# The first norm of a hybrid network taken in token rows ahead of the turn

## The chip, the cores and the metric

The kernel runs on one core of one Trainium2 chip. The metric is the device time of one execution in microseconds. Busy time, granted clock of TensorE and transfers are those of one profiled execution.

## What is computed

A network of two layers over 1,024 tokens of width 1,024, all in 32-bit floats. The part that matters here is its very start, the norm of the input and the first product with `hy_w_in`:

```
def rms_norm(x, w):
    xf = x.astype(jnp.float32)
    y = xf * lax.rsqrt(jnp.mean(xf * xf, axis=-1, keepdims=True) + EPS)
    return (y * w.astype(jnp.float32)).astype(x.dtype)
...
    h = x
    for layer in range(DEPTH):
        e = layer // 2
        y = rms_norm(h, norm_mix[layer])
        if layer % 2 == 0:
            y = hybrid_mixer(y, hy_w_in[e], ...)     # begins with y @ w_in
        else:
            y = nsa_mixer(y, nsa_w_in[e], ...)
        h = h + y
        h = h + conv_ffn(rms_norm(h, norm_ffn[layer]), ...)
    return rms_norm(h, norm_final)
```

Each token's row is divided by its root mean square, and each of its 1,024 features is then scaled by a gain. The raw `x` is needed again, as the residual, only after the mixer.

## The kernel before

Activations lie turned in SBUF: features on the 128 partitions, tokens along the row. `H` holds 8 such tiles (MT = 8, `H[:, m, :]`) of 128 features by 1,024 tokens. Products are made in units. A unit is one block of 128 output features; TensorE goes over i = 0 to 7 and for each i issues six matmuls of 512 columns. Both factors are split into an upper and a lower part (`WH`, `WL` of the weights, `YH`, `YL` of the normed activations), and three products of the parts are summed. GpSimd (POOL) splits the weights, `WH` (line 473) and `WL` (line 476), one unit of weights at a time into one of two slots; SyncE (SP) loads them into `WR` (line 376). Unit n's split waits for the end of unit n-1 on TensorE once both slots are in use, and the load of unit n waits for the split of unit n-2.

The start runs in this order. SP loads `x` as 8 tiles of 128 tokens into `Z`, then two small gate weight blocks (`GWR`), then the weights of units 0 and 1. The ACT queue issues 14 small parameter loads (`par_pieces`) and 6 small vector loads. TensorE turns the parameters (line 1876), VectorE (DVE) copies them to `PTF` (lines 1220, 1221). TensorE turns raw `x` (line 1883), 8 transposes for each m, into two pairs of PSUM banks; ACT copies the even tiles to `H` (line 803), DVE the odd ones (line 1224). Then ACT squares each tile (line 756), DVE adds the squares (lines 1135, 1137), TensorE sums over the partitions (line 1862), ACT takes the root (line 758), DVE the reciprocal (line 1143), and TensorE spreads the factor over all partitions (line 1869). Per tile m DVE then scales (line 1151), ACT makes `YH` (line 763) and POOL makes `YL` (line 498), through two temporary tiles. Unit 0 follows tile by tile; behind it TensorE makes the gate columns (line 1895), then unit 1, the turned gates, the key squares (line 2080), unit 2 and so on.

Seven level masks `LV` (128x128 each, lines 1247 to 1249) are made by DVE after the norm. The turned raw input `H` is spilled to DRAM as `xt_scratch` (line 404) as soon as the turns are evacuated, and SP issues the weights of unit 2 behind the spill.

There is no planner: each engine follows its own written order, and semaphores join them.

Of the kernel before, what the change touches and what calls it, by code (L numbers as in the profile page):

```python
# [6 lines left out]
def hybrid_nsa_program(nc, x, norm_mix, norm_ffn, norm_final, hy_w_in, gdn_conv, gdn_a_log, gdn_dt_bias,  # L7
# [6 lines left out]
    P = 128  # L14
# [29 lines left out]
    with ctx:  # L44
# [154 lines left out]
        SQ_READY, SQ_USED, SS_READY = (0, MT + 3 * (MT - 1)), (0, MT + 3 * (MT - 2)), (0, 1 + 3 * 2)  # L199
# [26 lines left out]
        (w_split, gemm_done, psum_free, x_loaded, par_loaded, vec_loaded, gw_loaded, gw_split, consts, par_t, pt_ready,  # L226
         xt_ready, xt_used, sq_ready, sq_used, ss_ready, rt_ready, yf_ready, yh_ready, y_ready, rstd_ready, rb_ready,
         spilled, restored_first, restored, xt_used_odd, w_hi, act_chain, dve_chain, pool_chain) = [sem(n) for n in (
             "w_split gemm_done psum_free x_loaded par_loaded vec_loaded gw_loaded gw_split consts par_t pt_ready "
             "xt_ready xt_used sq_ready sq_used ss_ready rt_ready yf_ready yh_ready y_ready rstd_ready rb_ready "  # L230
             "spilled restored_first restored xt_used_odd w_hi act_chain dve_chain pool_chain").split()]
        (tap_ready, conv_act, key_sq, key_ss, key_scale, key_root, gp_ready, sm_a, sm_v, gam_ready, lv_ready, ij_ready) = [sem(n) for n in (
            "tap_ready conv_act key_sq key_ss key_scale key_root gp_ready sm_a sm_v gam_ready lv_ready ij_ready").split()]
# [126 lines left out]

        block = ctx.enter_context(nc.Block())
# [3 lines left out]
        def _(sp):  # L365
            for tt in range(TT):
                sp.dma_start(Z[:, tt, :], x[0, chunk(tt), :]).then_inc(x_loaded, 16)
            w_in = hy_w_in[0].rearrange("(k p) n -> p k n", p=P)
            sp.dma_start(GWR[:, :, 0:8], w_in[:, :, 2048:2056]).then_inc(gw_loaded, 16)
            sp.dma_start(GWR[:, :, 8:16], w_in[:, :, 3592:3600]).then_inc(gw_loaded, 16)  # L370
# [30 lines left out]
            sp.wait_ge(xt_ready, MT)  # L401
# [49 lines left out]
        def _(pool):  # L451
# [42 lines left out]
            def y_lower(r, y0):  # L494

                for m in range(MT):
                    pool.wait_ge(yh_ready, r * MT + m + 1)
                    pool.tensor_tensor(YL[:, m, :], X[:, 17 + m % 2, :], YH[:, m, :].bitcast(f32),
                                       ALU.subtract).then_inc(y_ready, 1)

# [7 lines left out]

            splits(U_QKV, 2)
            gate_split(32, 16)  # L510
            y_lower(0, 0)
# [32 lines left out]
            pool.wait_ge(lv_ready, 1)  # L544
# [195 lines left out]
        def _(act):  # L740
# [7 lines left out]
            def norm(r, n0=None):  # L748
                for m in range(MT):
                    if n0 is None:  # L750
                        act.wait_ge(xt_used if m % 2 == 0 else xt_used_odd, m // 2 + 1)
                    else:
                        act.wait_ge(psum_free, n0 + m + 1)
                    if m >= 2:
                        act.wait_ge(sq_used, SQ_USED[r] + m - 1)
                    act.activation(X[:, 16 + m % 2, :], H[:, m, :], ACT.Square).then_inc(sq_ready, 1)
                act.wait_ge(ss_ready, SS_READY[r] + 1)
                act.activation(RSTD[:, :], PS[:, 4, 0:TT], ACT.Sqrt, scale=1.0 / DM, bias=EPSC[:, 0:1]).then_inc(rt_ready, 1)

            def norm_upper(r):  # L760
                for m in range(MT):
                    act.wait_ge(yf_ready, r * MT + m + 1)
                    act.activation(YH[:, m, :], X[:, 17 + m % 2, :], ACT.Copy).then_inc(yh_ready, 1)

            def half_norm(k, n0):

                for m in range(MT - 1):
                    act.wait_ge(psum_free, n0 + m + 1)
                    if m >= 3:
                        act.wait_ge(sq_used, MT + 6 * k + m - 2)  # L770
                    act.activation(X[:, 16 + m % 2, :] if m else PSF[:, 6 * HALF:8 * HALF], H[:, m, :], ACT.Square).then_inc(sq_ready, 1)
                act.wait_ge(nh_res, k + 1)
                act.wait_ge(sq_used, MT + 6 * k + 5)
                act.activation(X[:, 17, tok_half(0)], H[:, MT - 1, tok_half(0)], ACT.Square).then_inc(nh_sq, 1)

                def root(a):
                    act.wait_ge(ss_ready, 1 + 2 * k + a + 1)
# [4 lines left out]
                for a in range(2):  # L782
                    for m in range(MT):
                        act.wait_ge(yf_ready, MT + (2 * k + a) * MT + m + 1)
# [7 lines left out]
            for dst, src in par_pieces:  # L792
                act.dma_start(dst, src).then_inc(par_loaded, 16)
            for dst, src, lo in ((ALOG, gdn_a_log, 0), (ALOG, ssd_a_log, GH), (DTB, gdn_dt_bias, 0), (DTB, ssd_dt_bias, GH)):
                n = src.shape[1]
                act.dma_start(dst[:, lo:lo + n], src[0].partition_broadcast(P)).then_inc(vec_loaded, 16)
            for half in range(2):
                act.dma_start(DSK[half * 64:half * 64 + 64, :], ssd_d[0, half::2].partition_broadcast(64), allow_slow_non_contiguous=True).then_inc(vec_loaded, 16)


            for m in range(0, MT, 2):
                act.wait_ge(xt_ready, m + 1)
                act.activation(H[:, m, :], gemm_ps(0), ACT.Copy).then_inc(xt_used, 1)
            norm(0)
            norm_upper(0)

# [25 lines left out]
            for n in range(7):  # L832
# [22 lines left out]
                if n < 4:  # L855
                    act.wait_ge(conv_act, n + 1)
                    if n == 0:
                        act.wait_ge(spilled, 16)
                    if n >= 2:
                        act.wait_ge(key_ss, n - 1)  # L860
                    act.activation(X2(HF, 4 + n % 2), X[:, QKV[n], :], ACT.Square).then_inc(key_sq, 1)
# [259 lines left out]
        def _(dve):  # L1121
# [7 lines left out]
            def norm_sums(r, m):  # L1129
# [3 lines left out]
                dve.wait_ge(sq_ready, SQ_READY[r] + m + 1)  # L1133
# [5 lines left out]
                dve.wait_ge(sq_used, SQ_USED[r] + m + 1)  # L1139

            def norm_factor(r):
                dve.wait_ge(rt_ready, r + 1)
                dve.reciprocal(RSTD[:, :], RSTD[:, :]).then_inc(rstd_ready, 1)
                dve.wait_ge(rb_ready, r + 1)

            def norm_apply(r, wcol, y0):
                norm_factor(r)
                for m in range(MT):
                    if m >= 2:
                        dve.wait_ge(y_ready, y0 + m - 1)  # L1150
                    dve.scalar_tensor_tensor(out=X[:, 17 + m % 2, :], in0=H[:, m, :], scalar=PTF[:, wcol + m:wcol + m + 1],
                                             in1=PSF[:, 4 * HALF:6 * HALF], op0=ALU.mult, op1=ALU.mult).then_inc(yf_ready, 1)

            def half_residual(k, n0, wcol):

                def add_square(m):
                    dve.wait_ge(sq_ready, MT + 7 * k + m + 1)
                    dve.tensor_tensor(PSF[:, 6 * HALF:8 * HALF], PSF[:, 6 * HALF:8 * HALF], X[:, 16 + m % 2, :], ALU.add).then_inc(sq_used, 1)
                    dve.wait_ge(sq_used, MT + 6 * k + m)
# [5 lines left out]
                def factor(a):  # L1165
                    dve.wait_ge(rt_ready, 1 + 2 * k + a + 1)
                    dve.reciprocal(RSTD[:, 4 * a:4 * a + 4], RSTD[:, 4 * a:4 * a + 4]).then_inc(rstd_ready, 1)

                def apply(a, m):
                    if m == 0:  # L1170
                        dve.wait_ge(rb_ready, 1 + 2 * k + a + 1)
# [50 lines left out]
            for m in range(1, MT, 2):  # L1222
                dve.wait_ge(xt_ready, m + 1)
                dve.tensor_copy(H[:, m, :], gemm_ps(1)).then_inc(xt_used_odd, 1)

            for m in range(MT):
                norm_sums(0, m)
            norm_apply(0, C_MIX, 0)
# [15 lines left out]
            dve.wait_ge(y_ready, MT)  # L1244
            link(dve.tensor_scalar(LT, UT[:, :], -1.0, 1.0, ALU.mult, ALU.add))
            for l in range(7):
                link(dve.tensor_scalar(XI[:, 1, :], XI[:, 0, :], l, None, ALU.logical_shift_right))
                link(dve.tensor_copy(LV[:, l, :], XI[:, 1, :]))
                ins = dve.scalar_tensor_tensor(out=LV[:, l, :], in0=LV[:, l, :], scalar=1.0, in1=LT,
                                               op0=ALU.is_equal, op1=ALU.mult)  # L1250
                if l < 6:
                    link(ins)
                else:
                    ins.then_inc(lv_ready, 1)
            dve.wait_ge(pt_ready, 2)
# [84 lines left out]
            for n in range(7):  # L1340
                qkv_taps(n)
                if n == 0:
                    dve.wait_ge(gt_ready, 1)
                    dve.wait_ge(spilled, 16)
                    dve.tensor_copy(X2(HF, 7)[0:16], PSF[0:16, 6 * HALF:8 * HALF]).then_inc(gt_sb, 1)
# [26 lines left out]
                if n == 4:  # L1372
# [4 lines left out]
                    link(dve.tensor_tensor(BR2, BETA[:, :, 0:GH], KEYR2, ALU.mult))  # L1377
                    differences(0)
# [162 lines left out]
            def final_gain(m):  # L1541

                dve.wait_ge(sq_ready, SQ_READY[1] + m + 1)
                dve.tensor_scalar(H[:, m, :], H[:, m, :], PTF[:, C_FIN + m:C_FIN + m + 1], None, ALU.mult).then_inc(fin_ready, 1)

            def residual(n0):
                for m in range(MT):
# [228 lines left out]
        def _(pe):  # L1776
# [26 lines left out]
            def half_spread(k, a):  # L1803
                pe.wait_ge(rstd_ready, 1 + 2 * k + a + 1)
# [54 lines left out]
            def norm_sum(r):  # L1859
                pe.wait_ge(sq_used, SQ_USED[r] + MT)  # L1860
# [3 lines left out]
                if r == 1:  # L1864
                    return

                pe.wait_ge(rstd_ready, r + 1)
                for tt in range(TT):
                    ins = pe.matmul(PSF[:, 4 * HALF + tt * P:4 * HALF + (tt + 1) * P], RSTD[:, tt:tt + 1].broadcast_to([P, P]), IDENT[:, :],
                                    start=True, stop=True)  # L1870
                ins.then_inc(rb_ready, 1)
# [6 lines left out]
            pe.wait_ge(x_loaded, 16 * TT)  # L1878
            for m in range(MT):
# [643 lines left out]
```

## Time and profile before

| | |
|---|---|
| median of the runs | 3157.39 us (3147.24, 3157.39, 3164.39) |
| the profiled execution: its own time | 3148.27 us |
| its span | 3146.6 us, 1.7 us less than its own time |
| mean granted clock of TensorE | 0.97 |
| busy: TensorE, VectorE, ScalarE, GpSimd | 2922.7, 1237.2, 952.5, 1402.7 us |
| TensorE stops turning raw `x` | 27.2 us after the span's start |
| first matmul of unit 0 | 52.8 us |
| first gate column | 70.9 us |

The last three lines are read from the timeline of the start. They part the start into the turn of the raw input, the norm, and unit 0.

### The profile page before, as it was taken

How to read it: one execution, taken by the hardware profiler on the slowest of the kernel's cores; microseconds unless marked ns; L12 is line 12 of the kernel's file. 1: busy time of each engine (PE TensorE's matmuls, PEld its weight loads, DVE VectorE, ACT ScalarE, POOL GpSimd, SP SyncE). 2: the span in 40 equal slices, each digit the busy share in tenths (PEclk: the TensorE clock that was granted, in tenths of full speed). 3: DMA queues.
4: the chain of work that ended last, by engine and by line, in shares of the span. 5: the costliest groups of instructions: out<-in, count | busy, mean ns of one | idle time of the engine just before them, and what ended most of it. 6: DMA issues, size and time to landing. Idle time of an engine off the chain costs nothing. (4 is left out here: it accounts for less than half of the span.)

```text
span 3146.6 us, 43234 instructions
## 1 busy us (share of the span) xinstructions
PE 2922.7 (93%) x17295; PEld 2350.4 (75%) x17295; DVE 1237.2 (39%) x1991; ACT 952.5 (30%) x1567; POOL 1402.7 (45%) x908
## 2 busy tenths in 40 slices
PE   5998999989999999999995888789979999999998
PEld 3887878877888888887874556556667888888887
DVE  4455463524331331333004676644434331331334
ACT  3434442322330120112012554666723320210211
POOL 4354434555444444445522343444445444444442
PEclk8999999989999999999997998999989999999999
DMA  4110011021111111111123000000011111111111
GB/s 141 38 28 2 15 34 47 15 87 47 47 47 47 53 44 50 47 49 47 47 54 90 1 1 1 1 1 1 2 38 43 47 50 50 47 43 50 53 43 71
DMA packets 212558, 127.57 MB, mean 41 GB/s; under 512 B 9016, under 2 KB 208189, under 8 KB 212285
## 3 DMA queue, kind: packets, MB, share of 16 engines
q1 hardware_dynamic: 210608, 125.25, 13.6%
q8 instruction: 103, 1.69, 0.2%
q10 hardware_dynamic: 1805, 0.28, 0.1%
q14 instruction: 42, 0.34, 0.0%
HBM read 112.94 MB, written 8.39 MB: 39 GB/s over the span
## 5 line engine op out<-in xcount | busy, mean ns | idle before, releaser
L473 POOL TENSOR_TENSOR WH<-WR,ONES 128x1024 fp32r<-128x1024 f32 (+1 forms) x194 | 457.7, 2359 | 1121.9 <-PE PS L1789 1036.6
L1789 PE MATMUL PS<-YH,WH 128*128 128x512 f32 x2032 | 631.9, 392 | 30.5 <-DVE YL L1764 16.6
L1789 PE MATMUL PS<-YL,WH 128*128 128x512 f32 x2032 | 628.3, 390 | 0.0
L1789 PE MATMUL PS<-YH,WL 128*128 128x512 f32 x2032 | 627.6, 390 | 0.0
L476 POOL TENSOR_TENSOR WL<-WR,WH 128x1024 fp32r<-128x1024 f32 (+1 forms) x194 | 462.3, 2383 | 15.2
L1789 PEld LDWEIGHTS PS<-YH,WH 128*128 128x128 f32 x2032 | 381.9, 189 | 114.5 <-DVE YL L1764 16.8
L1569 DVE SCALAR_TENSOR_TENSOR X<-PS,PTF,X 128x1023 f32<-128x1023 f32 (+1 forms) x176 | 225.6, 1282 | 561.3 <-ACT X L1048 548.5
L1789 PEld LDWEIGHTS PS<-YL,WH 128*128 128x128 f32 x2032 | 383.1, 189 | 80.2
L1789 PEld LDWEIGHTS PS<-YH,WL 128*128 128x128 f32 x2032 | 382.9, 188 | 80.2
L1048 ACT ACTIVATE X<-PS,PTF 128x1024 f32<-128x1024 f32 x88 | 106.2, 1207 | 829.6 <-PE PS L1789 823.5
L1100 ACT ACTIVATE Z<-PS 128x512 f32<-128x512 f32 (+2 forms) x336 | 171.2, 540 | 162.0 <-PE PS L2443 161.2
L1789 PE MATMUL PS<-MH,WH 128*128 128x512 f32 x690 | 212.9, 390 | 0.0
L1789 PE MATMUL PS<-ML,WH 128*128 128x512 f32 x690 | 212.5, 389 | 0.0
L1789 PE MATMUL PS<-MH,WL 128*128 128x512 f32 x690 | 212.4, 389 | 0.0
L2422 PE MATMUL PS<-X 64*128 64x512 f32 (+3 forms) x768 | 156.5, 514 | 55.8 <-DVE STAT L1710 54.4
L703 POOL TENSOR_SCALAR X<-X,STAT,SM 128x640 f32<-128x640 f32 (+7 forms) x171 | 135.7, 802 | 138.0 <-DVE STAT L1721 138.0
L2462 PE MATMUL PS<-Z,X 128*64 128x128 f32 x2112 | 156.1, 287 | 3.5 <-DVE Z L1662 2.3
L2443 PE MATMUL PS<-IDENT,X 128*128 128x128 f32 (+1 forms) x799 | 138.4, 296 | 17.4 <-POOL X L695 9.2
L2422 PEld LDWEIGHTS PS<-X 64*128 64x128 f32 x768 | 66.6, 195 | 115.9 <-DVE STAT L1710 70.0
L1789 PEld LDWEIGHTS PS<-MH,WH 128*128 128x128 f32 x690 | 129.2, 188 | 28.2 <-DVE ML L1578 1.6
L1789 PEld LDWEIGHTS PS<-ML,WH 128*128 128x128 f32 x690 | 129.5, 188 | 27.0
L1789 PEld LDWEIGHTS PS<-MH,WL 128*128 128x128 f32 x690 | 129.5, 188 | 27.0
(379 smaller groups left out, 3875.1 us busy)
## 6 DMA issues: line engine op xcount, KB each, us to landing
WR<-in_ffn_w_up_dram SPq DMA_DIRECT2D x88, 512.0 KB, 3.8
WR<-in_hy_w_in_dram SPq DMA_DIRECT2D x28, 512.0 KB, 3.8
WR<-in_ffn_w_down_dram SPq DMA_DIRECT2D x32, 448.0 KB, 3.5
WR<-in_ffn_w_down_dram SPq DMA_DIRECT2D x16, 512.0 KB, 3.7
WR<-in_nsa_w_in_dram SPq DMA_DIRECT2D x14, 512.0 KB, 3.7
Z<-in_x_dram SPq DMA_DIRECT2D x8, 512.0 KB, 7.3
xt_scratch<-H SPq DMA_DIRECT2D x1, 4096.0 KB, 12.1
WR<-in_hy_w_out_dram SPq DMA_DIRECT2D x8, 512.0 KB, 3.7
```

Of the source, the lines that this page charges most:

```text
L473: pool.tensor_tensor(WH[:, slot, 0:k, :], WR[:, slot, 0:k, :], ONES[:, :].unsqueeze(1).broadcast_to([P, k, P]), ALU.mult).then_inc(w_hi, 1)
L476: pool.tensor_tensor(WL[:, slot, 0:k, :], WR[:, slot, 0:k, :], WH[:, slot, 0:k, :].bitcast(f32), ALU.subtract).then_inc(w_split, 1)
L703: pool.tensor_scalar(score_buf(p, i, 0, w), score_buf(p, i, 0, w), STAT[:, 2, n % 8:n % 8 + 1], GATE[:, qt, gate:gate + 1], ALU.mult, ALU. ...
L1048: act.activation(X[:, 16 + s, :], gemm_ps(s), ACT.Identity, scale=PTF[:, bass.ds(j + tap, 1)], bias=PTF[:, bass.ds(j + (C_FBIAS + l * 2 * ...
L1100: act.activation(PTR[g % len(PTR)][0:rows, 0:w], PS[0:rows, 4 + g % 2, 0:w], ACT.Copy).then_inc(pt_sb, 1)
L1569: dve.scalar_tensor_tensor(out=X[:, 16 + s, d:], in0=gemm_ps(s)[:, 0:SEQ - d], scalar=PTF[:, bass.ds(j + tap, 1)], in1=X[:, 16 + s, d:], o ...
L1789: ins = pe.matmul(PS[:, 2 * slot + a, :], w[:, slot, i, :], y[:, i, a * HALF:(a + 1) * HALF], start=(i == 0 and w is WH and y is hi), stop ...
L2422: ins = pe.matmul(gemm_ps(i)[:, a:e], X[part, h // 2, chunk(qt)], X[part, kt, first * P + a:first * P + e], start=True, stop=True)
L2443: ins = pe.transpose(PS[0:rows, 4 + g % 2, (k - 4 * i) * P:(k - 4 * i + 1) * P], src, IDENT[:, :])
L2462: ins = pe.matmul(PS[head_part(k), 6 + p % 2, 0:P], X[:, (VS, VW)[b], (first + t) * P + (h // JH) * DH:(first + t) * P + (h // JH) * DH + DH],
```

## The change

1. `x` goes to `X[:, 8:16]` and not to `Z`; the first four tiles and the last four have a semaphore each. Six of the 14 parameter loads move from the ACT queue to SP, behind `x`. The gate weights move on SP behind the weights of units 0 and 1. The vector loads move into ACT's loop over `YH`.
2. The squares are summed along the token's row, over the free dimension: tiles 0, 2, 4, 6 on DVE (`tensor_tensor_reduce`), tiles 1, 3, 5, 7 on ACT (Square with `accum_out`). One root and one reciprocal follow; the root's table is loaded ahead by a dummy activation. The partition sums and the spreading on TensorE go.
3. Rows are scaled by their factor in place of later multiplication: five tiles on DVE, three on ACT, into `X[:, 0:8]`. These normed rows are turned by TensorE, through three pairs of PSUM banks.
4. For each m ACT makes `YH` straight from the turned tile with the gain as its scale, DVE makes `YL` from the same tile, and then one level mask. POOL makes no `YL` at this place. POOL's first weight split waits until DVE's five normed tiles are ready.
5. TensorE issues turn m and then step m-2 of unit 0. When unit 0 is done it turns raw `x`, evacuated as before; the gate columns and the spill come behind that.
6. The scratch for key squares and gate rows moves from `H` to `X`, so these don't wait for the spill.

```
-                sp.dma_start(Z[:, tt, :], x[0, chunk(tt), :]).then_inc(x_loaded, 16)
+                sp.dma_start(X[:, 8 + tt, :], x[0, chunk(tt), :]).then_inc(x_loaded if tt < 4 else x_loaded_b, 16)
+            for dst, src in par_pieces[PAR_ACT:]:
+                sp.dma_start(dst, src).then_inc(par_loaded, 16)
...
             qkv_columns(0, 2)
-            sp.wait_ge(xt_ready, MT)
+            sp.dma_start(GWR[:, :, 0:8], w_in[:, :, 2048:2056]).then_inc(gw_loaded, 16)
+            sp.dma_start(GWR[:, :, 8:16], w_in[:, :, 3592:3600]).then_inc(gw_loaded, 16)
+            sp.wait_ge(xt_ready, 2 * MT)
...
+            pool.wait_ge(yf_ready, len(XN_DVE))
             splits(U_QKV, 2)
             gate_split(32, 16)
-            y_lower(0, 0)
...
+            act.wait_ge(consts, 3)
+            act.activation(STAT[:, 0, 0:1], EPSC[:, 0:1], ACT.Sqrt).then_inc(sq_ready, 1)
+            for tt in SQ_ACT:
+                act.wait_ge(x_loaded_b if tt >= 4 else x_loaded, 64)
+                act.activation(Z[:, 8 + tt, :], X[:, 8 + tt, :], ACT.Square, accum_out=RSTD[:, tt:tt + 1]).then_inc(sq_ready, 1)
+            act.wait_ge(sq_ready, 1 + len(SQ_ACT))
+            act.wait_ge(sq_used, SQU0)
+            act.activation(RSTD[:, :], RSTD[:, :], ACT.Sqrt, scale=1.0 / DM, bias=EPSC[:, 0:1]).then_inc(rt_ready, 1)
+            act.wait_ge(par_t, 1)
+            act.wait_ge(rstd_ready, 1)
+            for tt in XN_ACT:
+                act.activation(X[:, tt, :], X[:, 8 + tt, :], ACT.Identity, scale=RSTD[:, tt:tt + 1], bias=0.0).then_inc(sq_ready, 1)
+            act.wait_ge(pt_ready, 2)
+            for m in range(MT):
+                act.wait_ge(xt_ready, m + 1)
+                act.activation(YH[:, m, :], turned_x(m), ACT.Identity, scale=PTF[:, C_MIX + m:C_MIX + m + 1], bias=0.0).then_inc(yh_ready, 1)
...
+            for tt in range(TT):
+                if tt not in SQ_ACT:
+                    dve.wait_ge(x_loaded_b if tt >= 4 else x_loaded, 64)
+                    dve.tensor_tensor_reduce(out=Z[:, 8 + tt, :], in0=X[:, 8 + tt, :], in1=X[:, 8 + tt, :], scale=1.0, scalar=0.0,
+                                             op0=ALU.mult, op1=ALU.add, accum_out=RSTD[:, tt:tt + 1]).then_inc(sq_used, 1)
...
+            for tt in XN_DVE:
+                dve.tensor_scalar(X[:, tt, :], X[:, 8 + tt, :], RSTD[:, tt:tt + 1], None, ALU.mult).then_inc(yf_ready, 1)
+            link(dve.tensor_scalar(LT, UT[:, :], -1.0, 1.0, ALU.mult, ALU.add))
             for m in range(MT):
-                norm_sums(0, m)
-            norm_apply(0, C_MIX, 0)
+                dve.wait_ge(yh_ready, m + 1)
+                dve.scalar_tensor_tensor(out=YL[:, m, :], in0=turned_x(m), scalar=PTF[:, C_MIX + m:C_MIX + m + 1],
+                                         in1=YH[:, m, :].bitcast(f32), op0=ALU.mult, op1=ALU.subtract).then_inc(y_ready, 1)
+                if m < 7:
+                    link(dve.tensor_scalar(XI[:, 1, :], XI[:, 0, :], m, None, ALU.logical_shift_right))
+                    link(dve.tensor_copy(LV[:, m, :], XI[:, 1, :]))
+                    ins = dve.scalar_tensor_tensor(out=LV[:, m, :], in0=LV[:, m, :], scalar=1.0, in1=LT, op0=ALU.is_equal, op1=ALU.mult)
...
+            def turn_normed(m):
+                if m == 0:
+                    pe.wait_ge(yf_ready, len(XN_DVE))
+                    pe.wait_ge(sq_ready, SQ0)
...
+                if m >= 3:
+                    pe.wait_ge(y_ready, m - 2)
+                for tt in range(TT):
+                    ins = pe.transpose(turned_x(m)[:, chunk(tt)], X[:, tt, chunk(m)], IDENT[:, :])
+                ins.then_inc(xt_ready, 1)
...
+            for m in range(MT):
+                turn_normed(m)
+                if m >= 2:
+                    first_unit(m - 2)
+            for i in range(MT - 2, MT):
+                first_unit(i)
             for m in range(MT):
+                if m == 0:
+                    pe.wait_ge(y_ready, MT)
                 if m >= 2:
                     pe.wait_ge(xt_used if m % 2 == 0 else xt_used_odd, m // 2)
                 for tt in range(TT):
-                    ins = pe.transpose(gemm_ps(m % 2)[:, chunk(tt)], Z[:, tt, chunk(m)], IDENT[:, :])
+                    ins = pe.transpose(ps_pair(m % 2)[:, chunk(tt)], X[:, 8 + tt, chunk(m)], IDENT[:, :])
                 ins.then_inc(xt_ready, 1)
```

`first_unit(i)` waits for the weights of unit 0 (at i = 0) and for `y_ready` i+1, and issues the six matmuls of step i.

## Rows read from the trace of the kernel before

**Rows 1.** The page, busy time of each engine over the span.
```profile
PE 2922.7 (93%) x17295; PEld 2350.4 (75%) x17295; DVE 1237.2 (39%) x1991; ACT 952.5 (30%) x1567; POOL 1402.7 (45%) x908
```

**Rows 2.** Windows: length, busy PE, PEld, DVE, ACT, POOL, granted clock, DMA share, GB/s.
```profile
30.00:53.00 23.00, 7.17 (x33) 6.95 (x34) 11.56 (x11) 9.89 (x10) 7.75 (x5) 0.58 0.57 205
53.00:71.30 18.30, 14.69 (x49) 10.16 (x50) 8.83 (x13) 6.34 (x6) 16.23 (x7) 0.87 0.00 1
...
82.00:130.00 48.00, 48.00 (x244) 40.43 (x242) 18.91 (x29) 17.70 (x20) 14.32 (x6) 1.00 0.13 34
```

**Rows 3.** Transfers of the start: loads of `x`, the spill, unit 2's weights behind it.
```profile
L367 SPq DMA_DIRECT2D Z<-in_x_dram x8: 399/438/572, 0.8 to 4.3; - x8
DMA to landing us min/median/max: 4.0/7.3/10.8
...
xt_scratch<-H SPq DMA_DIRECT2D x1, 4096.0 KB, 12.1
...
DMA to landing us min/median/max: 13.6/13.6/13.6
```

**Rows 4.** Timeline of the start: start, length, engine, line, operation.
```profile
15.05 1.28 PE L1876 MATMUL PS<-IDENT,X 128*128 128x128 f32 x5 [15.05 <-DMA X<-in_cmp_pos_v_dram]
16.26 4.68 PE L1883 MATMUL PS<-IDENT,Z 128*128 128x128 f32 x24
16.44 0.67 DVE L1220 COPY PTF<-PS 128x485 f32<-128x485 f32 x1 [13.66 <-PE PS L1876]
21.25 1.97 PE L1883 MATMUL PS<-IDENT,Z 128*128 128x128 f32 x16 [0.31 <-DVE H L1224]
27.20 1.22 DVE L1224 COPY H<-PS 128x1024 f32<-128x1024 f32 x1 [1.19 <-PE PS L1883]
44.40 3.46 PE L1869 MATMUL PS<-IDENT,RSTD 128*128 128x128 f32 x16 [0.67 <-DVE RSTD L1143]
52.84 1.19 PE L1789 MATMUL PS<-YH,WH 128*128 128x512 f32 x2 [4.98 <-POOL YL L498]
70.94 0.09 PEld L1895 LDWEIGHTS PS<-YH,GWH 128*16 128x16 f32 x1
82.30 0.62 PE L1789 MATMUL PS<-YH,WH 128*128 128x512 f32 x2
83.67 0.61 PE L1789 MATMUL PS<-YH,WH 128*128 128x512 f32 x2
95.68 0.72 PE L1789 MATMUL PS<-YH,WH 128*128 128x512 f32 x2
```

**Rows 5.** Timeline: where VectorE and GpSimd instructions overlap.
```profile
28.68 1.63 DVE L1135 TENSOR_TENSOR X<-X 128x1024 f32<-128x1024 f32 x1 [0.25 <-ACT X L756]
29.31 3.22 POOL L476 TENSOR_TENSOR WL<-WR,WH 128x1024 fp32r<-128x1024 f32 x1
71.49 2.40 POOL L473 TENSOR_TENSOR WH<-WR,ONES 128x1024 fp32r<-128x1024 f32 x1 [1.86 <-PE PS L1789]
71.62 2.35 DVE L1247 TENSOR_SCALAR SM<-SM 128x128 int32<-128x128 int32 x1
74.01 2.44 DVE L1248 CAST X<-SM 128x128 f32<-128x128 int32 x1
```

**Rows 6.** Forms nearest to the new ones: grouped, or shortest/median/longest in ns.
```profile
L1710 DVE CUSTOM_DVE_ANT_0 X<-PS,Z 128x1024 f32<-128x1024 f32 x11 | 13.1, 1222 | 13.0 <-PE PS L2422 7.7 <-PE PS L2443 5.4
L1151 DVE SCALAR_TENSOR_TENSOR X<-H,PTF,PS 128x1024 f32<-128x1024 f32 x8 | 10.2, 1279 | 11.6 <-POOL YL L498 8.0 <-PE PS L1869 3.6
L1088 ACT ACTIVATE X<-X,STAT 128x1024 f32<-128x1024 f32 x11 | 12.5, 1146 | 0.6 <-DVE STAT L1710 0.6
L1544 DVE TENSOR_SCALAR H<-H,PTF x8: 752/2042/2497, 3066.3 to 3126.6; 128x1024 f32<-128x1024 f32 x8
L1249 DVE SCALAR_TENSOR_TENSOR X<-X x7: 291/292/293, 70.4 to 79.9; 128x128 f32<-128x128 f32 x7
L1247 DVE TENSOR_SCALAR SM<-SM x7: 226/227/2354, 69.9 to 79.4; 128x128 int32<-128x128 int32 x7
```

More of the change, by code:

```diff
@@ L790, in half_norm @@
                         root(1)
-            for dst, src in par_pieces:
+            for dst, src in par_pieces[:PAR_ACT]:
                 act.dma_start(dst, src).then_inc(par_loaded, 16)
[L794 to L798, printed above, removed]
+            act.wait_ge(consts, 3)
@@ L801, in _ @@
             for m in range(0, MT, 2):
[L802 to L805, printed above, removed]
+                act.wait_ge(xt_ready, MT + m + 1)
+                act.activation(H[:, m, :], ps_pair(0), ACT.Copy).then_inc(xt_used, 1)
             def conv_tap(n, tile, wcol, bcol):
@@ L1138, in norm_sums @@
                     ins.then_inc(sq_used, 1)
[L1139 to L1152, printed above, removed]
+                dve.wait_ge(sq_used, SQ_USED + m + 1)
             def half_residual(k, n0, wcol):
                 def add_square(m):
-                    dve.wait_ge(sq_ready, MT + 7 * k + m + 1)
+                    dve.wait_ge(sq_ready, SQ0 + 7 * k + m + 1)
                     dve.tensor_tensor(PSF[:, 6 * HALF:8 * HALF], PSF[:, 6 * HALF:8 * HALF], X[:, 16 + m % 2, :], ALU.add).then_inc(sq_used, 1)
-                    dve.wait_ge(sq_used, MT + 6 * k + m)
+                    dve.wait_ge(sq_used, SQU0 + 6 * k + m)
                 def sum_last(a):
@@ L1243, in _ @@
             conv_no = [0]
[L1244 to L1255, printed above, removed]
+            for m in range(1, MT, 2):
+                dve.wait_ge(xt_ready, MT + m + 1)
+                dve.tensor_copy(H[:, m, :], ps_pair(1)).then_inc(xt_used_odd, 1)
             def qkv_taps(n):
@@ L1863, in norm_sum @@
                 ins.then_inc(ss_ready, 1)
[L1864 to L1871, printed above, removed]
             pe.wait_ge(consts, 3)
@@ L1877, in _, with first_unit @@
             ins.then_inc(par_t, 1)
-            pe.wait_ge(x_loaded, 16 * TT)
-            for m in range(MT):
+            def turn_normed(m):
+                if m == 0:
+                    pe.wait_ge(yf_ready, len(XN_DVE))
+                    pe.wait_ge(sq_ready, SQ0)
+                if m == 2:
+                    pe.wait_ge(pt_ready, 2)
+                if m >= 3:
[3 more added lines that the diff above has]
+                ins.then_inc(xt_ready, 1)
+            def first_unit(i):
+                if i == 0:
+                    pe.wait_ge(w_split, 1)
+                pe.wait_ge(y_ready, i + 1)
+                for w, y in ((WH, YH), (WH, YL), (WL, YH)):
+                    for a in range(2):
+                        ins = pe.matmul(PS[:, a, :], w[:, 0, i, :], y[:, i, tok_half(a)], start=(i == 0 and w is WH and y is YH),
+                                        stop=(i == MT - 1 and w is WL))
+                if i == MT - 1:
+                    ins.then_inc(gemm_done, 1)
+            for m in range(MT):
+                turn_normed(m)
[6 more added lines that the diff above has]
+                    pe.wait_ge(y_ready, MT)
                 if m >= 2:
@@ L2484, in _ @@
             ffn(1, 2)
[L2485 removed]
+            norm_sum()
             pe.wait_ge(fin_ready, MT)
```

113 lines of the change are left out of this document (57 added, 56 removed).

## The prediction

> **What bounds the kernel now.** The page comes first: TensorE is busy for 93% of the span, the others for less than half [rows 1]. Windows by stage then show where TensorE is not busy. From 82 us on it has no gap at all (48.00 of 48.00 us, clock 1.00), while from 30 to 53 us it works 7.17 of 23 us at a clock of 0.58 [rows 2]. So the first 71 us are a prologue: everything behind the first gate column at 70.94 us is bound by TensorE, and what the start saves is saved at the end, one for one, if nothing that the dense stage needs arrives later than before. The timeline gives the prologue's parts [rows 4]: parameters and raw turns until 28.4 us (27.20 + 1.22), squares, sums, root and spreading until 47.9 us (44.40 + 3.46), then 23 us in which three engines pass each tile on and unit 0 follows (first matmul 52.84, first gate column 70.94). The number to forecast is the new time of the first gate column.
>
> **The change, part by part.**
>
> *Loads.* The eight tiles of `x` are issued from 0.8 to 4.3 us, and the last lands 10.8 us after its issue, at 15.1 us [rows 3]. They were first in SP's queue already. Only small parameter pieces run beside them, so I keep 15.1; the bounds are 14 and 16. The parameters were waited for until 15.05 [rows 4]; six pieces now stand behind `x` on SP, and I put their turn at 16.1 to 17.4. The weights of units 0 and 1 are issued ahead of the gate weights and are needed only at 22 us; no cost.
>
> *Squares.* Half of them run on tiles that land by 9 us and are hidden. The last four, two on each engine, start at 15.1. The nearest rows are a DVE reduce form of 1.22 us and an ACT form with a per-row scale and a sum of 1.15 us [rows 6]; with reading out the sum I allow 1.3 us each: done at 17.7. The root runs while DVE copies `PTF` (0.67 us [rows 4] and a smaller copy). Factor ready at 18.8. This replaces 19.5 us of squares, sums and spreading (28.4 to 47.9).
>
> *Scaled rows.* Five `tensor_scalar` on DVE at the shortest time of that form, 0.75 us [rows 6]: 3.8 us, since POOL is held back until they are done. Three on ACT at 1.15: 3.5 us. Ready at 22.6 us.
>
> *Turns.* Sixteen transposes take 1.97 us late in the raw turn, 3.46 us at half clock, and the very first 24 take 4.68 us [rows 4]. So a turn costs 0.98 us at speed and about 1.75 us after a rest. Turn 0 is done at 24.4, `YH` 0 on ACT at 25.6, `YL` 0 on DVE (PSUM and one SBUF input, 1.28 us as line 1151 [rows 6]) at 26.9.
>
> *POOL against DVE.* This is the term that I weigh most. POOL now starts its four weight splits and two gate splits at about 22.8 us, just when DVE begins its chain. They are 4 x 2.4 us [rows 5] and about 2.6 us: busy until 35.3. In the trace, a mask instruction of 0.23 us [rows 6] that meets a weight split lasts 2.35 us, the next one 2.44 [rows 5]: each is held until the split that is running ends. Behind `YL` m stand three such instructions, linked one to the next, and `YL` m+1 stands behind them in DVE's order. The third kind (line 1249, both inputs in SBUF) shows only 0.29 us, but never met POOL [rows 6]; a nearer row for two SBUF inputs is line 1135 at 28.68, which ran past the end of a split and made the next split last 3.22 us and not 2.4 [rows 5]. So I let all three be held. Mask 0: first instruction until 27.7, second until 30.1, third until 32.6. `YL` 1 is ready at 33.9. Mask 1 loses until 35.3, then POOL is through (its next split waits for the end of unit 0), and `YL` 2 is ready at 37.2. From there on a tile costs 1.28 + 0.23 + 0.23 + 0.29 and three hand-overs, 2.15 to 2.2 us: `YL` 7 at 48.1.
>
> The Trainium skill (SBUF — State Buffer, "Who interferes with whom") says the same and more: of a DVE instruction in a two-port mode and a GpSimd instruction, the one that starts first has the shared pair of ports for its whole length, and DVE instructions with two SBUF inputs contend with GpSimd's reads too. The traces of the first two kinds agree (2.35 and 2.44 us against 0.23); for the third kind no row shows it on its own form. By the rule the third instruction is held as in my sum; if it were free, `YL` 1 would come 2.4 us sooner and the gain be about 1 to 2 us more. The rule speaks against putting the masks here.
>
> *Unit 0.* A step of six matmuls takes 1.37 us at speed (82.30 to 83.67 [rows 4]), a turn 0.98: together 2.35 us for a tile, just above DVE's 2.2. Waiting for `YL` 1 and 2, TensorE rests some 3.5 us at about 30 to 34, and its clock may fall for a few us; in the trace it fell to half after the raw turns ended at 27.2 [rows 2, 4]. With one step and one turn at half speed it catches up about as DVE ends. End of unit 0: 49.6 if only DVE counts; I take 50.5.
>
> *Raw turns.* These now stand between unit 0 and the gate columns, which need their PSUM banks. Two turns 2.0 us, one DVE copy 1.2 us, then three pairs more at the old cadence of 2.4 us (a DVE copy 1.22 and its wait 1.19 [rows 4]): 10.5 us, first gate column at 61.1. All of this is on the path; before, they overlapped nothing either, so here the order costs nothing but also saves nothing.
>
> *Sum.* 70.9 - 61.1 = 9.8 us. Removed: partition sums and spreading, two separate passes, POOL's 2.4 us per tile. Given back: the masks (6 us of DVE time on the path and some 7 us held).
>
> *What comes later than before.* The spill and unit 2's weights wait for the raw turns: issue at about 61 us and not 28.5, landing 13.6 us later [rows 3] at 75. The splits take until 80. Unit 2 begins 24.7 us after the first gate column (70.94 to 95.68 [rows 4]), so at 85.8: 5.7 us of cover. If it were gone, each further us would be one of the whole time. Mask use, key squares and gate rows have no new wait. ACT's six small DMA issues in the `YH` loop fit beside DVE's 2.2 us a tile.
>
> Against the profiled execution, 3148.3 us (span 3146.6 and 1.7 around it), the sum gives 3138.5. The median of the runs shown is 3157.4, 9 us above that execution; from it I forecast 3147.6.
>
> **Rivals.**
>
> 1. *The masks are not held*, or POOL and DVE pass each other cheaply, and TensorE stays at speed. Then tiles run at 2.2 us from `YL` 0 on: `YL` 7 at 42, unit 0 done at 43.5, first gate column at 54.1. Gain 17 us, time 3140.5; with an earlier landing of `x`, 18. For: line 1249 never shows a hold. Against: the two holds at 71 and 74 us.
> 2. *TensorE's clock stays at half through the whole start.* After `YL` 1 there remain four turns at 1.75 and seven steps at about 2.5 (1.37 times the turns' ratio): 24.5 us, unit 0 done at 58.4; the raw turns then take 15 us, as two turns at 1.75 us outlast a copy. First gate column at 73.5, and part of it at half clock: 3 to 6 us slower than before, 3160 to 3163. It decides once unit 0 ends past 60.3 us. For: the clock 0.58 from 30 to 53 us. Against: from 53 to 71 us the mean is 0.87 [rows 2] with the same kind of work, and here TensorE would be without a rest.
> 3. *The raw turns and the spill cost what the norm saves*: unit 2's weights land over 10 us after the spill's own 12.1 us, or POOL's splits come late, and unit 2 waits. 10 us beyond the cover brings no change, 3157. Against: the load's 13.6 us were measured behind the same spill [rows 3].
>
> **How the numbers follow.** Half a per cent is 15.8 us, about what measurements of this kernel can tell. The forecast (gain 5 to 14 us) has a chance of 0.61, rival 1 has 0.25, rival 2 has 0.07, rival 3 and less of a gain than 5 us have 0.07. Only most of rival 1 is faster by over 0.5%, and runs spread by up to 8 us around their median: faster 0.24, same 0.72, slower 0.04. The range goes from rival 1 with its earlier landing and some of that spread, 3134, to no change with as much, 3160.
>
> **What would show it.** In the profile of the changed kernel: `x` landed at 15, five DVE scalings of 0.75 us up to 22.6, POOL starting just then; mask 0's instructions at about 2.4 us each and a hole of 6 to 7 us between the first two `YL`; then `YL` every 2.2 us; raw turns beginning at 50.5; gate columns at 61; unit 2 with no wait for its split. Wrong would be: scalings at twice the time, mask instructions all near 0.23 us (rival 1), a clock of 0.5 past 40 us (rival 2), or TensorE idle before unit 2 (rival 3).

## The result, and the profile after

The changed kernel takes 3138.94 us in the median of 13 runs, the kernel before 3151.44 us in the median of 13. The ratio is 0.995, with a 95% interval from 0.9934 to 0.9967. That is 12.5 us between the medians, where the sum said 9.8 (the interval of the ratio allows 10.4 to 20.8 us). The profiled executions differ by 12.8 us in their spans, 3146.6 and 3133.8. The forecast time was 3147.6 us.

The sum was made for one event, the first gate column. In the kernel before it stood at 70.94 us and the first step of unit 1 at 82.30 [rows 4]. Now they stand at 57.7 and 68.86: 13.2 and 13.4 us earlier. The rest of the kernel, from unit 1 to the end, can be compared by windows. First the kernel before, then the changed one, each parted at its own start of unit 1, at the start of the attention stage and at its end (the windows end at those events):

```profile
82.30:1697.50 1615.20, 1547.10 (x8867) 1287.77 (x8865) 570.38 (x712) 403.25 (x520) 732.87 (x414) 0.98 0.16 45
1697.50:2281.00 583.50, 496.92 (x4460) 341.74 (x4462) 341.67 (x998) 355.33 (x852) 252.00 (x300) 0.93 0.01 1
2281.00:3146.60 865.60, 834.91 (x3776) 689.60 (x3772) 286.92 (x236) 167.99 (x171) 379.84 (x168) 0.98 0.16 49
```

```profile
68.86:1684.30 1615.44, 1548.74 (x8867) 1289.50 (x8865) 567.83 (x711) 401.19 (x518) 738.09 (x416) 0.98 0.16 46
1684.30:2269.70 585.40, 501.22 (x4460) 344.98 (x4462) 341.92 (x998) 355.74 (x852) 252.93 (x300) 0.93 0.01 1
2269.70:3133.80 864.10, 834.85 (x3776) 689.71 (x3772) 286.98 (x236) 168.01 (x171) 379.95 (x168) 0.99 0.16 49
```

The first column behind the window is its length: the three parts are as long as before, within 2 us each (0.2 and 1.9 us longer, 1.5 us shorter). In these two executions, what was gained in the start arrived at the end. That it fits to 0.6 us is partly luck: a second execution of the same changed kernel, shown further down, has an attention stage shorter by 5.7 us.

The start itself, from the timeline of the changed kernel, in the places of [rows 4] and [rows 5]:

```profile
14.42 1.23 DVE L1220 CUSTOM_DVE_ANT_0 Z<-X 128x1024 f32<-128x1024 f32 x1 [3.13 <-DMA X<-in_x_dram]
...
17.79 3.40 DVE L1229 TENSOR_SCALAR X<-X,RSTD 128x1024 f32<-128x1024 f32 x5
...
21.25 5.04 PE L1884 MATMUL PS<-IDENT,X 128*128 128x128 f32 x24 [4.40 <-DVE X L1229]
...
23.71 2.37 POOL L487 TENSOR_TENSOR WL<-WR,WH 128x1024 fp32r<-128x1024 f32 x1
24.55 1.28 DVE L1233 SCALAR_TENSOR_TENSOR YL<-PS,PTF,YH 128x1024 fp32r<-128x1024 f32 x1 [3.22 <-ACT YH L806]
...
25.75 0.41 DVE L1236 TENSOR_SCALAR SM<-SM 128x128 int32<-128x128 int32 x1
26.03 2.40 POOL L484 TENSOR_TENSOR WH<-WR,ONES 128x1024 fp32r<-128x1024 f32 x1
...
26.19 2.32 DVE L1237 CAST X<-SM 128x128 f32<-128x128 int32 x1
...
28.50 2.34 POOL L487 TENSOR_TENSOR WL<-WR,WH 128x1024 fp32r<-128x1024 f32 x1
28.54 2.45 DVE L1238 SCALAR_TENSOR_TENSOR X<-X 128x128 f32<-128x128 f32 x1
...
30.79 0.35 POOL L501 CAST GWH<-SM 128x128 fp32r<-128x128 f32 x1
31.03 1.28 DVE L1233 SCALAR_TENSOR_TENSOR YL<-PS,PTF,YH 128x1024 fp32r<-128x1024 f32 x1
...
32.37 1.02 PE L1893 MATMUL PS<-YH,WH 128*128 128x512 f32 x2 [3.71 <-DVE YL L1233]
...
33.07 1.28 DVE L1233 SCALAR_TENSOR_TENSOR YL<-PS,PTF,YH 128x1024 fp32r<-128x1024 f32 x1
...
35.11 1.28 DVE L1233 SCALAR_TENSOR_TENSOR YL<-PS,PTF,YH 128x1024 fp32r<-128x1024 f32 x1
...
36.53 1.12 ACT L806 ACTIVATE YH<-PS,PTF 128x1024 fp32r<-128x1024 f32 x1 [6.72 <-PE PS L1884]
...
44.42 1.28 DVE L1233 SCALAR_TENSOR_TENSOR YL<-PS,PTF,YH 128x1024 fp32r<-128x1024 f32 x1 [0.18 <-ACT YH L806]
...
47.24 1.91 PE L1910 MATMUL PS<-IDENT,X 128*128 128x128 f32 x16
```

What to see: the squares of the last tiles start at 14.4 (the input has landed), the scaled rows are ready at 21.2, and between the first two `YL` (24.55 and 31.03) there are 6.5 us. In this hole stand two mask instructions of 2.32 and 2.45 us, each ending within 0.15 us of a weight split; the second form takes 0.29 us alone [rows 6], the first 0.23 us (26.30, in the kernel with later splits below). `YL` itself, with one input in PSUM and one in SBUF, kept its 1.28 us beside the split that began at 23.71. TensorE waits 3.71 us for the hole. Then `YL` 2 and 3 follow 2.04 us apart, the later ones wait for `YH`, `YL` 7 begins at 44.42, and the raw turns begin at 47.24.

Put beside the parts of the start before: loading, raw turns, sums and spreading took until 47.9 us, and the chain of tiles with unit 0 took 23.0 us more. Now the load takes until 14.4, squares with root 3.4 us, scaling 3.4 us, the chain with unit 0 26.0 us (21.2 to 47.24) and the raw turns 10.5 us. So most of the gain is that of the sums, 19.5 us replaced by 6.8. Load and raw turns together take 24.9 us and not 28.4, and the chain of tiles, with the hole in it, is 3 us longer than before. This is read from rows; no run takes the row sums alone, or GpSimd's `YL`, back.

The clock of TensorE around that wait, in windows of the changed kernel (length, busy PE, PEld, DVE, ACT, POOL, granted clock, DMA share, GB/s):

```profile
26.00:28.65 2.65, 2.65 (x17) 2.03 (x15) 2.58 (x3) 1.20 (x2) 2.57 (x3) 1.00 0.05 2
28.65:32.30 3.65, 0.00 (x1) 0.00 (x0) 3.61 (x3) 1.11 (x1) 2.95 (x3) 1.00 0.02 1
32.30:34.90 2.60, 2.54 (x7) 1.85 (x8) 2.43 (x8) 0.00 (x0) 0.00 (x0) 0.56 0.00 0
34.90:36.50 1.60, 1.60 (x10) 1.60 (x9) 1.56 (x3) 0.00 (x0) 0.00 (x0) 0.64 0.00 0
36.50:47.20 10.70, 10.70 (x60) 8.94 (x60) 7.64 (x16) 4.46 (x4) 0.00 (x0) 1.00 0.03 3
```

After 3.7 us without work TensorE is at the lower of its two levels (1.2 and not 2.4 GHz) for one step and one turn, and back at full speed from about 36.1 us: the granted clock is 0.70 from 35.8 to 36.2 and 1.00 from 36.2 on. From 34.9 us on it has no gap in which it could make this up.

### The profile page after: what moved, and what is told of

The parts are those of the page before. It is cut to its first block and busy times, and to the rows that moved or that the text cites. A ratio compares the mean times of both kernels' runs of the same rounds, so it can differ in the third digit from the quotient of the medians.

```text
span 3133.8 us, 43294 instructions
## 1 busy us (share of the span) xinstructions
PE 2927.8 (93%) x17327; PEld 2355.8 (75%) x17327; DVE 1234.2 (39%) x1997; ACT 951.8 (30%) x1570; POOL 1382.7 (44%) x900
## 5 line engine op out<-in xcount | busy, mean ns | idle before, releaser
L1794 PE MATMUL PS<-YH,WH 128*128 128x512 f32 x2016 | 625.4, 392 | 21.9 <-DVE YL L1769 16.6
```

The lines of the kernel that those rows point to most:

```text
L1794: ins = pe.matmul(PS[:, 2 * slot + a, :], w[:, slot, i, :], y[:, i, a * HALF:(a + 1) * HALF], start=(i == 0 and w is WH and y is hi), stop ...
```

## The experiments

All are edits of the changed kernel. The measure is the start of unit 1 in the profile (82.30 us before, 68.86 changed), since single executions of one kernel differ by several us far behind it, as the last experiment shows. Six of the eight were executed once only (3132.3 to 3146.1 us), and these times decide nothing; early masks have five executions, both edits together six.

| kernel | unit 0 ends | unit 1 begins | against changed |
|---|---|---|---|
| changed | 47.24 | 68.86 | 0 |
| masks while the input lands | 42.3 | 63.95 | -4.9 |
| later splits held back | 42.2 | 63.77 | -5.1 |
| unit 0 behind all turns | 50.4 | 71.97 | +3.1 |
| raw turns ahead of the scaling | 57.8 | 68.92 | +0.1 |
| splits as soon as weights land | 49.1 | 70.72 | +1.9 |
| all squares on VectorE | 50.9 | 72.52 | +3.7 |
| raw turns between gate columns | 47.2 | 65.41 | -3.5 |
| early masks and raw turns between | 42.4 | 60.60 | -8.3 |

**Masks while the input lands.** The seven masks and the tile `LT` are made ahead of the squares.

```
             link(dve.tensor_tensor(XI[:, 0, :], XI[:, 0, :], XI[:, 1, :], ALU.bitwise_xor))
+            dve.wait_ge(consts, 3)
+            link(dve.tensor_scalar(LT, UT[:, :], -1.0, 1.0, ALU.mult, ALU.add))
+            for m in range(7):
+                link(dve.tensor_scalar(XI[:, 1, :], XI[:, 0, :], m, None, ALU.logical_shift_right))
+                link(dve.tensor_copy(LV[:, m, :], XI[:, 1, :]))
...
             for m in range(MT):
                 dve.wait_ge(yh_ready, m + 1)
...
-                if m < 7:
-                    link(dve.tensor_scalar(XI[:, 1, :], XI[:, 0, :], m, None, ALU.logical_shift_right))
-                    link(dve.tensor_copy(LV[:, m, :], XI[:, 1, :]))
...
```

> The seven level masks and their helper tile are made by VectorE while x is still landing (2.8 to 8.8 us), not between the YL tiles. Theory (masks held behind GpSimd's weight splits set the pace of the first two YL tiles): the hole between YL 0 and YL 1 closes, TensorE then goes at 2.35 us a tile from 26 us on, unit 0 ends near 42.0 us instead of 47.24 and unit 1 begins near 63.7 us instead of 68.86, a gain of 5 us. Rival (the masks only filled time in which VectorE would have waited for YH or TensorE anyway): unit 1 within 1 us of 68.86.

Unit 1 begins at 63.95 us, 4.9 us earlier. The hole is closed, and the cadence is now TensorE's and ACT's. From the timeline of this kernel:

```profile
24.46 1.28 DVE L1243 SCALAR_TENSOR_TENSOR YL<-PS,PTF,YH 128x1024 fp32r<-128x1024 f32 x1 [3.27 <-ACT YH L806]
...
26.11 1.28 DVE L1243 SCALAR_TENSOR_TENSOR YL<-PS,PTF,YH 128x1024 fp32r<-128x1024 f32 x1 [0.36 <-ACT YH L806]
...
39.49 1.28 DVE L1243 SCALAR_TENSOR_TENSOR YL<-PS,PTF,YH 128x1024 fp32r<-128x1024 f32 x1 [0.97 <-ACT YH L806]
...
42.32 1.91 PE L1912 MATMUL PS<-IDENT,X 128*128 128x128 f32 x16
```

VectorE now waits 0.97 us a tile for `YH`, and the tiles follow each other in TensorE's 2.25 us. Timed against the kernel before (five runs of it): ratio 0.9938, interval 0.9908 to 0.9968. This overlaps the changed kernel's interval, so the 4.9 us are shown in the profile of the start and not in the whole time.

**Later splits held back.** The masks stay where the change put them.

```
-            splits(U_QKV, 2)
+            splits(U_QKV, 1)
+            pool.wait_ge(y_ready, MT)
+            splits(U_QKV + 1, 1)
             gate_split(32, 16)
```

> The masks stay between the YL tiles, but GpSimd holds the split of unit 1's weights and of the gate weights until all eight YL are ready. Theory (being held is the whole cost of the masks, their own 0.8 us a tile lies beside TensorE's 2.35): unit 0 ends near 42.2 us, unit 1 begins near 63.9, as in the kernel with early masks. Rival (the masks' own length is on the path too): unit 0 ends 2 to 5 us later than with early masks.

Unit 1 at 63.77 us, within 0.2 us of the kernel with early masks. The timeline of this kernel has the masks at their own length, but for the first instruction, which still meets a split (0.41 us):

```profile
25.86 0.41 DVE L1238 TENSOR_SCALAR SM<-SM 128x128 int32<-128x128 int32 x1
26.30 0.23 DVE L1239 CAST X<-SM 128x128 f32<-128x128 int32 x1
26.57 0.29 DVE L1240 SCALAR_TENSOR_TENSOR X<-X 128x128 f32<-128x128 f32 x1
...
26.89 1.28 DVE L1235 SCALAR_TENSOR_TENSOR YL<-PS,PTF,YH 128x1024 fp32r<-128x1024 f32 x1
```

So being held behind GpSimd is the whole price of the masks, within these 0.2 us; their own 0.8 us a tile is hidden, since `YL` with its mask goes every 2.04 us and TensorE's tile takes 2.25. Two edits that share nothing but the missing overlap give the same 5 us.

**Unit 0 behind all turns.** The interleaving is undone.

```
             for m in range(MT):
                 turn_normed(m)
-                if m >= 2:
-                    first_unit(m - 2)
-            for i in range(MT - 2, MT):
+            for i in range(MT):
                 first_unit(i)
```

> Unit 0 stands behind all eight normed turns and not between them. Theory (the interleaving lets TensorE work while VectorE makes YL): turn 7 ends near 39.5 us, the eight steps take 11 us at speed and up to 2 more after a rest, unit 0 ends at 50.5 to 52.5 instead of 47.24, unit 1 begins at 72 to 74. Rival (VectorE's pace sets the end either way): unit 1 within 1 us of 68.86.

Unit 1 at 71.97, the lower edge of what was expected. The first step of unit 0 starts at 39.35 and its six matmuls take 1.5 us, full speed: the slow spell had fallen on the turns before it (the granted clock is 0.50 from 32.3 to 35.3). The interleaving is worth 3.1 us.

**Raw turns ahead of the scaling.** The raw turns go into banks 0 to 3 and are evacuated before the rows are scaled. The spill then starts at 28.4 us.

```
+            for m in range(MT):
+                if m == 0:
+                    pe.wait_ge(x_loaded, 64)
+                    pe.wait_ge(x_loaded_b, 64)
+                if m >= 2:
+                    pe.wait_ge(xt_used if m % 2 == 0 else xt_used_odd, m // 2)
+                for tt in range(TT):
+                    ins = pe.transpose(gemm_ps(m % 2)[:, chunk(tt)], X[:, 8 + tt, chunk(m)], IDENT[:, :])
+                ins.then_inc(xt_ready, 1)
             for m in range(MT):
                 turn_normed(m)
...
+            for m in range(1, MT, 2):
+                dve.wait_ge(xt_ready, m + 1)
+                dve.tensor_copy(H[:, m, :], gemm_ps(1)).then_inc(xt_used_odd, 1)
             dve.wait_ge(rstd_ready, 1)
             for tt in XN_DVE:
```

> The raw turns and their evacuations stand ahead of the scaling, as in the kernel before, with the rest of the change kept. Theory (the raw turns cost some 10 us wherever they stand in the start): the scaled rows are ready near 31.3 us and not 21.2, and the gate columns follow unit 0 at once at about 57.4, so unit 1 begins at 68 to 71 us, within 2 us of 68.86. Rival (putting them behind unit 0 is itself the gain): unit 1 begins over 4 us later, at 73 or more.

Unit 1 at 68.92, 0.06 us from the changed kernel. From its timeline:

```profile
16.73 4.17 PE L1905 MATMUL PS<-IDENT,X 128*128 128x128 f32 x24
...
28.26 3.39 DVE L1232 TENSOR_SCALAR X<-X,RSTD 128x1024 f32<-128x1024 f32 x5
```

The scaling is 10.5 us later (28.26 and not 17.79), which is what the raw turns cost behind unit 0 (47.24 to 57.74). Turning the raw input behind unit 0 is therefore no part of the gain.

**Splits as soon as weights land.** The line `pool.wait_ge(yf_ready, len(XN_DVE))` is left out.

> GpSimd does not wait for the scaled rows: it splits unit 0's weights as soon as they land, near 19 to 20 us. Theory (a two-port VectorE instruction and a GpSimd instruction exclude each other): one or two of the five scalings last over 2 us instead of 0.7, the normed rows are ready 1 to 3 us later than 21.2, and the masks meet as many splits; unit 1 begins 0 to 2 us later than 68.86. Rival (the splits are only moved forward): unit 1 begins 1 to 2 us earlier.

```profile
16.58 2.62 POOL L484 TENSOR_TENSOR WH<-WR,ONES 128x1024 fp32r<-128x1024 f32 x1 [14.13 <-DMA WR<-in_hy_w_in_dram]
...
17.83 10.87 DVE L1228 TENSOR_SCALAR X<-X,RSTD 128x1024 f32<-128x1024 f32 x5
...
19.28 2.67 POOL L487 TENSOR_TENSOR WL<-WR,WH 128x1024 fp32r<-128x1024 f32 x1
21.93 2.78 POOL L484 TENSOR_TENSOR WH<-WR,ONES 128x1024 fp32r<-128x1024 f32 x1
24.79 2.67 POOL L487 TENSOR_TENSOR WL<-WR,WH 128x1024 fp32r<-128x1024 f32 x1
```

The mechanism came out as expected, its size did not: the weights had landed already at 16.6 us, not 19 to 20, and four of the five scalings were stretched, to 1.93 us and three times about 2.8; the fifth took 0.77. Together they took 10.87 us in place of 3.40. The two engines take turns, about one instruction each. The scaled rows are 7.5 us later, but unit 1 loses only 1.9 us, because the masks then meet no split and TensorE does not rest: from `YL` 0 to `YL` 7 it is 14.2 us (32.05 to 46.28) and not 19.9. The wait of GpSimd in the change is worth these 1.9 us.

**All squares on VectorE.** `SQ_ACT` is empty.

> All eight sums of squares on VectorE, none on ScalarE. Theory (the last four tiles' squares are on the path, the first four are hidden by the landing): two more of 1.15 us behind the landing, the root and all behind it 2.3 to 2.6 us later, unit 1 begins near 71.3 us. Rival (the wait for the parameters and their copies covers it): unit 1 within 1 us of 68.86.

Unit 1 at 72.52, 3.7 us later. The scaled rows are 2.4 us later, as expected: 2 x 1.15. So is the end of TensorE's wait (34.74 and not 32.37). The other 1.3 us were not expected, and lie behind it, in TensorE's clock. In this execution, after the same wait of 3.7 us:

```profile
34.70:37.30 2.60, 2.56 (x6) 2.04 (x7) 2.43 (x7) 0.00 (x0) 0.00 (x0) 0.50 0.00 0
37.30:38.90 1.60, 1.60 (x8) 1.43 (x7) 1.56 (x3) 0.00 (x0) 0.00 (x0) 0.50 0.00 0
38.90:41.00 2.10, 2.10 (x8) 1.73 (x7) 0.89 (x4) 1.11 (x1) 0.00 (x0) 0.54 0.00 0
```

The lower level lasted until about 40.8 us, 6.1 us after work resumed, and in the changed kernel 3.7 us. From the end of the wait on the work is the same, and it takes 16.2 us to the end of unit 0 and not 14.9.

**Raw turns between gate columns.** A turn stands before each group of six gate matmuls, into banks 4-5 and 2-3, and SP loads the weights of units 2 and 3 ahead of the spill.

```
                 for a in range(2):
                     for i in range(MT):
+                        if between is not None and i % 2 == 0:
+                            between(a * MT // 2 + i // 2)
...
-                    gate_columns(16)
+                    gate_columns(16, turn_raw)
+                    pe.wait_ge(xt_used, MT // 2)
+                    pe.wait_ge(xt_used_odd, MT // 2)
...
+            qkv_columns(2, 2)
             sp.wait_ge(xt_ready, 2 * MT)
```

> The raw turns stand between the gate columns, one after every six gate matmuls, in the bank pairs 4-5 and 2-3, and the weights of units 2 and 3 are loaded ahead of the spill. Theory (behind unit 0 the raw turns cost 10.5 us, of which 2.5 are waits for evacuations that other matmuls could fill): gate columns and turns together last 19 us, unit 1 begins near 66.3 us instead of 68.86. Rival (the turns' waits only move, or a late copy holds unit 1's banks): unit 1 within 1 us of 68.86.

Unit 1 at 65.41, 3.5 us earlier and 0.9 more than expected. Gate columns and turns together last 18.2 us (47.21 to 65.41) in place of 21.6. From the timeline of this kernel:

```profile
47.21 1.04 PE L1912 MATMUL PS<-IDENT,X 128*128 128x128 f32 x8
48.00 0.48 PE L1922 MATMUL PS<-YH,GWH 128*16 128x512 f32 x1
...
49.47 1.03 PE L1912 MATMUL PS<-IDENT,X 128*128 128x128 f32 x8
```

TensorE is busy in all of the 18.20 us, where behind unit 0 it was busy in 8.29 of 10.50: the 2.2 us of waits for evacuations are gone. The other 1.2 us come from the turns themselves: one that is followed at once by other matmuls holds TensorE for 0.79 us (47.21 to 48.00), and 0.98 us were counted.

**Both.** The two edits together.

> Early masks and raw turns between the gate columns together. Theory (the two costs are separate and add): unit 0 ends near 42, unit 1 begins near 61 us, 21 us ahead of the kernel before and 8 ahead of the changed one; time 0.993 of the kernel before. Rival (they overlap, or the dense stage takes it back): less than 6 us ahead of the changed kernel.

Unit 1 at 60.60, 8.3 us ahead of the changed kernel: the two gains (4.9 and 3.5) add. The ratio to the kernel before is 0.9932, interval 0.9906 to 0.9957; median 3134.29 us. The start of unit 1 does not tell all. In this execution TensorE fell to its lower level once more, in unit 2 and with no gap in its work; before it stood the 16 matmuls of one column for the key squares:

```profile
75.10:78.30 3.20, 3.20 (x9) 2.45 (x8) 2.55 (x6) 1.41 (x3) 1.60 (x1) 0.50 0.09 16
```

That costs about 1.6 us (an estimate: half of 3.2). The profiles of early masks, of the first one with later splits and of splits as soon as weights land have it too. The others have not, among them the second profiles of the kernels with held splits and with both edits, so it belongs to the execution and not to the kernel.

**The changed kernel and two versions again**, side by side, to see whether the whole time follows.

> The changed kernel again, beside the two below. Theory (all of its gain lies ahead of unit 1): unit 1 begins at 68.9 us within 0.2 us; the rest of the span, unit 1 to the end, lies where the other profiles have it, 3064 to 3077 us, with its spread between executions in the attention stage. Rival (the start changes the rest of the kernel too): the rest is on one side of the kernel before by more than that spread.

> GpSimd's splits held until the eight YL are ready, again and timed. Theory: unit 1 at 63.8 us, 18.5 us ahead of the kernel before, ratio 0.994, 0.0016 below the changed kernel's of the same call. Rival: no difference to the changed kernel in the ratio beyond its interval, although unit 1 begins 5 us earlier, because executions differ by more in the attention stage.

> Early masks and raw turns between the gate columns, again and timed. Theory: unit 1 at 60.6 us, 21.7 us ahead of the kernel before, ratio 0.993, 0.0026 below the changed kernel's of the same call. Rival: the ratio stays within 0.001 of the changed kernel's.

| kernel | unit 1 begins | span | attention stage | median | ratio, interval |
|---|---|---|---|---|---|
| changed | 68.94 | 3130.9 | 579.7 | 3139.67 | 0.9959, 0.994 to 0.9979 |
| splits held back | 63.50 | 3139.3 | 590.4 | 3137.08 | 0.9934, 0.9911 to 0.9957 |
| both | 59.89 | 3119.3 | 582.1 | 3133.63 | 0.993, 0.9907 to 0.9953 |

The start repeats within 0.8 us. The whole span of one execution does not follow it: the kernel with held splits is 5.4 us earlier at unit 1 and 8.4 us later at the end. The attention stage holds most of this. Its window in the changed kernel and in the one with held splits, in these executions:

```profile
1687.10:2266.80 579.70, 497.22 (x4460) 342.16 (x4462) 341.58 (x998) 355.67 (x852) 251.96 (x300) 0.94 0.01 1
```

```profile
1684.80:2275.20 590.40, 505.83 (x4460) 346.77 (x4462) 342.01 (x998) 355.31 (x852) 251.94 (x300) 0.92 0.01 1
```

Both have the same instructions and the same busy time on VectorE, ScalarE and GpSimd; the granted clock differs, 0.94 and 0.92, and the stage is 10.7 us longer at the lower one. The same kernel has 585.4 us there in its first profile and 579.7 in its second. The ratios fall in the order of the starts, but their intervals overlap: that the version with both edits beats the changed kernel is shown for the start (8.3 and 9.1 us) and is likely, not shown, for the whole time.

## Why the prediction held

**The path.** "What the start saves is saved at the end, one for one": 13.4 us at unit 1, 12.8 in the spans of the profiles, 12.5 between the medians. The windows above and the interval of the ratio (10.4 to 20.8 us) agree with it; they do not show it to the microsecond, since the attention stage alone differs by 5.7 us between two executions of the changed kernel.

**The sum.** It put the first gate column at 61.1 us; it came at 57.7, 3.4 us sooner. The difference builds up so: 1.4 us at the scaled rows, 1.6 at the end of `YL` 1, 2.9 at the end of `YL` 2, 3.3 at the end of unit 0, 3.4 behind the raw turns. The forecast time was 8.7 us too long: 2.7 us are the gain (9.8 and not 12.5), and 6.0 us are the kernel before, whose median over 13 runs is 3151.44 and not the 3157.39 of three. Those three also spread by 10.2 us around their median and not by 8.

**Loads, squares, scaling.** Scaled rows ready at 21.2 and not 22.6. The input landed at 14.4 and not 15.1, inside the bounds; five scalings took 3.40 us and not 3.8, since each lasts 0.75 us but the next starts 0.66 us behind it; squares and root took 3.4 us and not 3.7.

**POOL against DVE.** The mechanism was right, the third mask instruction with it: the form that had never met a split took 2.45 us, as the row of line 1135 [rows 5] and the Trainium skill's rule (SBUF — State Buffer, "Who interferes with whom") both had it. Its sizes were off in two places, both to the good. The first mask instruction came 0.3 us before a split ended, and was held only to 0.41 us. And the gate splits took 0.35 and 0.46 us, not 2.6 together, so mask 1 met nothing. That term was mis-sized by 1.8 us, 1.3 of them on the path. The hole between the first two `YL` was 6.5 us (forecast 6 to 7). What the sum calls given back is not right as it stands: the masks' own 6 us of VectorE time were not on the path, as the held splits show; the whole price of the masks was 5 us.

**Pace behind it.** `YL` 1 to `YL` 7 took 13.4 us, 2.23 a tile. The forecast of 2.15 to 2.2 came near by two errors that cancel. VectorE alone goes every 2.04 us (31.03, 33.07, 35.11), and it did not set the pace: from `YL` 4 on it waits for `YH`, which waits for a turn, and TensorE's tile takes 2.25 us, not 2.35. TensorE's clock did fall as said, but it was not caught up. Had VectorE kept its 2.04 us, as it does in the kernel whose splits are not held, `YL` 7 would have begun at 43.3 and not 44.42, so the slow spell cost about 1.2 us (an estimate from these rows). I had allowed 0.9 us for it, behind the last `YL`; it came ahead of it, and unit 0 ended 1.5 us behind the last `YL`.

**Raw turns.** 10.5 us forecast, 10.5 measured (47.24 to 57.74). That the order neither costs nor saves: 0.06 us by experiment.

**Unit 2's weights.** The split that waits for them starts at 72.90 and ends at 77.8; unit 2 begins at 82.26. The cover is 4.5 us, 5.7 were forecast.

**The rivals.** Rival 1 (masks not held) did not happen, but two kernels made it happen, and it was worth 5 us and not 7. Its own time was right: it puts the first gate column at 54.1, and with the scaled rows 1.4 us sooner that is 52.7; early masks have it at 52.82. The 7 us were too much because the sum for held masks was 2 us too long. Rival 2 fell: the lower clock lasted 3.7 us of work. Rival 3 fell by the cover above.

## What to carry to other kernels

Look for VectorE instructions whose inputs and output all lie in SBUF (here masks and scalings) in the stretch in which GpSimd works on SBUF, and move them out of it or hold GpSimd back there. Small instructions on a chain paid up to a whole GpSimd instruction each (0.23 and 0.29 us became 2.32 and 2.45), and this price doesn't show in their durations alone. When a prologue stands ahead of a stage in which TensorE has no gap, count to the first event of that stage and test edits by that event; here it repeated within 0.8 us where the whole time did not. Waits for evacuations between transposes can be filled with matmuls into other banks: here that was 2.2 us.

## What the runs showed of the hardware

VectorE and GpSimd alternated when both had instructions ready: five scalings of 0.75 us each became 10.87 us together, and four splits of 2.4 us became 2.62 to 2.78 us each.

The two instructions of the gate split took 1.28 and 1.34 us in the kernel before and 0.35 and 0.46 in the changed one, for the same 128x128 tile. Before, they ran beside VectorE's additions of squares (line 1137, both inputs in SBUF, 31.57 to 40.04 us), and where they meet scalings, in the kernel whose splits are not held, they took 0.74 and 0.78. So being held by VectorE is the likely reason; no run tests it alone, and GpSimd's spans are rough.

After one and the same wait of 3.7 us TensorE worked at its lower clock for 3.7 us in one execution and for 6.1 in another. A start that came 2.4 us later so cost 3.7. And the clock fell for some 3 us without any gap in TensorE's work, behind 16 matmuls of one column, in four of the 13 profiles.
